# Odd mixer: stacked running sums for the decay rows, one exponential a head, sums of squares tile by tile

## The reference

```python
# Conformer: val * sigmoid(gate), causal conv of 31 taps, layer norm over 512 channels, silu
u = _causal_dwconv(val * jax.nn.sigmoid(gate), conv_w, conv_b)
return jax.nn.silu(_layer_norm(u, ln_g, ln_b))

# Mamba-2 SSD: 16 heads of 64 in 2 groups, chunks of 128 tokens
a_cum = jnp.cumsum(dt_c * a_head.reshape(G, HG), axis=2)
seg = a_cum[:, :, :, None] - a_cum[:, :, None, :]
decay_ls = jnp.exp(jnp.where(causal, seg, -jnp.inf))
cb = jnp.einsum('bclgn,bcsgn->bclsg', c_c, b_c)
y_diag = jnp.einsum('bclsgh,bcsghp->bclghp', cb[..., None] * decay_ls, xdt)
...
y_off = jnp.einsum('bclgn,bcghpn,bclgh->bclghp', c_c, prev, jnp.exp(a_cum))
y = (y_diag + y_off) + d_skip * xs
y = y * jax.nn.silu(z)
yg = yg * lax.rsqrt(jnp.mean(jnp.square(yg), axis=-1, keepdims=True) + LN_EPS)   # per group of 512
```

## Time and profile before

| | us |
|---|---|
| median of 3 runs | 1790.54 (1789.36 to 1792.71) |
| the profiled execution | 1790.46 |
| its span | 1788.4 |
| PE busy (matmul) | 1684.4, 94% |
| DVE, ACT, POOL busy | 1015.6, 739.4, 139.2 |
| mean granted TensorE clock | 0.968 of 2.4 GHz |

### The profile page before, as it was taken

The page is one execution under the profiler, slowest core; times in us unless marked ns, Lnnn a source line. Parts: engine busy times, 40 slices in busy tenths (PEclk is TensorE's granted clock), DMA queues, the critical chain, the costliest instruction groups (busy, mean ns, idle before and its releaser), DMA issues.

```text
span 1788.4 us, 26739 instructions
## 1 busy us (share of the span) xinstructions
PE 1684.4 (94%) x10986; PEld 1397.2 (78%) x10986; DVE 1015.6 (57%) x1276; ACT 739.4 (41%) x1019; POOL 139.2 (8%) x155
## 2 busy tenths in 40 slices
PE   7998998989899999999998989899998999999996
PEld 6777897778677888888776766688887788888885
DVE  4589564664666543434488864455636755434346
ACT  4544543363425232324267744523634441423231
POOL 5110110000000000000025620000000000000000
PEclk9998999999999999999999999799999999999998
DMA  5220002344022333233232220053530233333231
GB/s 193 71 83 25 4 4 97 130 131 129 25 94 87 103 94 100 91 105 118 83 130 79 86 71 12 1 189 94 156 104 22 96 96 105 95 95 104 88 127 59
DMA packets 41161, 159.73 MB, mean 89 GB/s; under 512 B 4560, under 2 KB 4688, under 8 KB 39632
## 3 DMA queue, kind: packets, MB, share of 16 engines
q1 hardware_dynamic: 41040, 158.03, 28.1%
HBM read 153.81 MB, written 4.19 MB: 88 GB/s over the span
## 4 chain that ended last, share of the span: by engine, by line
PE 80%; DVE 13%; ACT 4%; issue 2%; DMA 0%; POOL 0%; SPq 0%; DVEq 0%; ACTq 0%; POOLq 0%
PE bank L569 24%; PE bank L571 23%; PE bank L570 23%; DVE w_lo L1664 2%; DVE h L1680 1%; PE bank L731 1%; PE bank L1067 1%; DVE nbh L1725 1%; PE bank L941 1%; DVE act_lo L1677 1%; ACT w_hi L1194 1%; PE bank L750 1%; PE bank L744 1%; DVE sconv L1680 1%; DVE lnst L1993 1%
## 5 line engine op out<-in xcount | busy, mean ns | idle before, releaser
L1664 DVE TENSOR_TENSOR w_lo<-w_raw,w_hi 128x1024 fp32r<-128x1024 f32 x263 | 326.8, 1244 | 312.5 <-ACT w_hi L1194 309.8
L569 PE MATMUL bank<-act_lo,w_hi 128*128 128x512 f32 x1048 | 418.1, 399 | 31.8 <-DVE w_lo L1664 16.2
L1194 ACT ACTIVATE w_hi<-w_raw 128x1024 fp32r<-128x1024 f32 x263 | 278.9, 1061 | 361.5 <-PE bank L571 347.4
L570 PE MATMUL bank<-act_hi,w_lo 128*128 128x512 f32 x1048 | 413.0, 394 | 0.0
L571 PE MATMUL bank<-act_hi,w_hi 128*128 128x512 f32 x1048 | 412.7, 394 | 0.0
L569 PEld LDWEIGHTS bank<-act_lo,w_hi 128*128 128x128 f32 x1048 | 200.2, 191 | 80.6 <-issue 18.0
L570 PEld LDWEIGHTS bank<-act_hi,w_lo 128*128 128x128 f32 x1048 | 200.2, 191 | 42.3 <-issue 1.2
L571 PEld LDWEIGHTS bank<-act_hi,w_hi 128*128 128x128 f32 x1048 | 199.9, 191 | 42.5
L569 PE MATMUL bank<-w_lo,aux_hi 128*128 128x512 f32 x576 | 224.5, 390 | 5.3 <-DVE act_lo L1677 5.3
L570 PE MATMUL bank<-w_hi,aux_lo 128*128 128x512 f32 x576 | 224.2, 389 | 0.0
L571 PE MATMUL bank<-w_hi,aux_hi 128*128 128x512 f32 x576 | 224.1, 389 | 0.0
(11 more groups left out here) (355 smaller groups left out, 2087.5 us busy)
## 6 DMA issues: line engine op xcount, KB each, us to landing
w_raw<-weights SPq DMA_DIRECT2D x263, 512.0 KB, 3.6
gb<-ln_rows SPq DMA_DIRECT2D x6, 1024.0 KB, 5.8
stage<-x_feat SPq DMA_DIRECT2D x4, 512.0 KB, 6.0
h<-x_tok SPq DMA_DIRECT2D x1, 2048.0 KB, 8.7
stage<-mem_feat SPq DMA_DIRECT2D x2, 1024.0 KB, 5.7
spill<-h SPq DMA_DIRECT2D x1, 2048.0 KB, 7.2
h<-spill SPq DMA_DIRECT2D x1, 2048.0 KB, 7.9
out<-h SPq DMA_DIRECT2D x4, 512.0 KB, 2.6
```

What stands on the lines that cost most here:

```text
L569: pe.matmul(o, whi, xlo, start=first, stop=False)
L570: pe.matmul(o, wlo, xhi, start=False, stop=False)
L1194: act.activation(w_hi[:, s], w_raw[:, s], ACT.Copy).then_inc(S("w_hi_done"), 1)
L1664: dve.tensor_tensor(w_lo[:, s], w_raw[:, s], f(w_hi[:, s]), ALU.subtract).then_inc(S("w_split"), 1)
```

## The change

The decay rows: the mask aside, one product per chunk of 128 tokens makes `a_cum[l] - a_cum[s]` at once. `from_sums` and `to_sums` hold the sums' high and low parts and constants stacked on 112 partitions; `head_row` (ACT) picks one head by a 0/1 scale per partition (`heads16`) into `head_sums`. One exponential of 512 columns per head then does. Rows go two pairs ahead of the scores. The sums of squares come tile by tile: the conformer's inside chunk 28 (`inside`, after every second of its eight pieces), the SSD's one pair behind the scores. `crb` follows pair 0, `conf_norm` (DVE) follows pairs 1 and 2, `conf_gate` (ACT) pairs 5 to 7. The output projection takes its inputs in another order (`SLOT1`, with the weight chunks in `SOURCE` to match), the first SSD group before the conformer. In the input projection the scan, `dt_tokens`, the four-instruction exponential block and the channel mean change their turns.

```diff
...
+                    12: [("free cacc", 0)], 15: [("stok", 2)], 16: [("free cacc", 1)], 18: [("slast", 1)],
                     20: [("sxt", 2)], 21: [("free cacc", 2), ("sxt", 2)], 22: [("sxt", 2)], 23: [("sxt", 2)],
-                    24: [("sbt", 2), ("scb", 2)], 25: [("free cacc", 3), ("sst", 2), ("cmean", 1)],
-                    26: [("sst", 2), ("yoff", 2)], 27: [("sst", 2), ("csum", 1)], 28: [("yoff", 2), ("crb", 1), ("sbc0", 2)]}
+                    24: [("sbt", 2), ("scb", 2)], 25: [("sst", 2)], 26: [("free cacc", 3), ("sst", 2), ("cmean", 1), ("yoff", 2)],
+                    27: [("sst", 2)], 28: [("yoff", 2)]}
...
-        TILES += [("yoff", 2)]
...
-        TILES += [("out1", 4), ("rsum1", 1), ("rbc1", 1), ("out1", 4)]
+            TILES += [(f"sbc{_h + 2}", 2)] * (_h < 6) + [(f"sy{_h}", 1)]
+            TILES += [("crb", 1)] * (_h == 0) + [("rsum", 1)] * (_h in (1, 5)) + [("rbc0", 1)] * (_h == 6)
+            TILES += [("free rsum", 0)] * (_h == 6)
+        TILES += [("out1", 4), ("rbc1", 1), ("free rsum", 1), ("out1", 4)]
...
-        acum_hi = sb("acum_hi", [16, T], F32R, at=aux_at + 12288)
-        acum_lo = sb("acum_lo", [16, T], F32R, at=aux_at + 14336)
+        HK = 112
+        from_sums = sb("from_sums", [HK, T], F32R, at=aux_at + 12288)
+        to_sums = sb("to_sums", [HK, T], at=aux_at + 14336)
+        sums_hi = sb("sums_hi", [16, T], F32R, at=aux_at + 8 * PW * 4)
+        head_sums = [sb("head_sums01", [HK, 2, T], F32R, at=after_p1 + 4 * (CP + T) * 4 + 8192),
+                     sb("head_sums23", [HK, 2, T], F32R, at=lru_at)]
+        SLOT1 = [4, 5, 6, 7, 0, 1, 2, 3, 8, 9, 10, 11]
...
+                if j == 2:
+                    pool.wait_ge(S("cval_out"), 4)
+                    pool.memset(to_sums[:], -1.0).then_inc(S("masks"), 1)
+                    pool.tensor_copy(from_sums[:], ones[0:HK, 0:1].to_broadcast([HK, T])).then_inc(S("masks"), 1)
...
                     hd = 2 * hp + q
+                    pe.wait_ge(S("s_head"), hd + 1)
                     o = take(f"sbc{hp}", q)
-                    head = identr[0:16, hd:hd + 1].to_broadcast([16, P])
-                    pe.matmul(o[:], head, acum_hi[:], start=True, stop=False)
-                    pe.matmul(o[:], head, acum_lo[:], start=False, stop=False)
-                    pe.matmul(o[:], identr[:], causalr[:], start=False, stop=True).then_inc(S("mixer_mm"), 1)
-
-            def token_sums(name, tiles):
-
-                o = take(name, 0)
+                    to_head = head_sums[hp % 2]
+                    for c in range(NSC):
+                        cols = slice(c * SC, c * SC + SC)
+                        pe.matmul(o[:, cols], from_sums[:, cols], to_head[:, q, cols], start=(c == 0), stop=False,
+                                  skip_group_check=True)
+                    pe.matmul(o[:], identr[:], causalr[:], start=False, stop=True, skip_group_check=True)\
+                        .then_inc(S("mixer_mm"), 1)
+
...
                 for c in range(NSC):
-                    for j in range(4):
-                        last = pe.matmul(o[:, c:c + 1], tiles(j)[:, c * SC:c * SC + SC], ones[:, 0:1], start=(j == 0),
-                                         stop=(j == 3))
-                last.then_inc(S("mixer_mm"), 1)
+                    last = pe.matmul(o[:, c:c + 1], tile[:, c * SC:c * SC + SC], ones[:, 0:1],
+                                     start=(first and c == 0), stop=(j == 3), skip_group_check=True)
...
+            def square_sums(hp):
+
+                g, j = divmod(hp, 4)
+                if j == 0:
+                    take("rsum", g)
+                pe.wait_ge(S("s_ysq"), hp + 1)
+                last = token_sums(bank("rsum", g), p1[:, XS + hp, PAD:PW], j, j == 0)
+                if j == 3:
+                    last.then_inc(S("rsum_mm"), 1)
...
             def at_26():
                 chunk_states(1)
+                channel_mean()
                 from_states(1)
...
+            def variance(k):
+
+                if k % 2:
+                    if k == 1:
+                        take("csum", 0)
+                    pe.wait_ge(S("c_sq"), k // 2 + 1)
+                    last = token_sums(bank("csum", 0), csq[:, k // 2], k // 2, k == 1)
+                    if k == KD - 1:
+                        last.then_inc(S("mixer_mm"), 1)
...
+            def odd_mixer():
+
+                from_states(3)
                 pe.wait_ge(S("masks"), 2)
                 decay_rows(0)
-
-            def odd_mixer():
-
-                from_states(3)
+                decay_rows(1)
                 for hp in range(8):
-                    if hp < 7:
-                        decay_rows(hp + 1)
+                    if hp < 6:
+                        decay_rows(hp + 2)
...
-                    if hp == 4:
-                        square_sums(0)
+                    if hp == 0:
+                        pe.wait_ge(S("c_rstd"), 1)
+                        across_features("crb", CROOT)
+                    if hp:
+                        square_sums(hp - 1)
...
-                                  between={13: dt_tokens, 18: dt_last, 20: lambda: values_to_tokens(0),
...
-                                           23: lambda: values_to_tokens(3), 24: keys_to_tokens, 25: at_25, 26: at_26,
-                                           27: at_27, 28: at_28}, place=PLACE1)
+                                           23: lambda: values_to_tokens(3), 24: keys_to_tokens, 25: lambda: chunk_states(0),
+                                           26: at_26, 27: lambda: chunk_states(2), 28: lambda: from_states(2)},
+                                  inside={28: variance}, place=PLACE1)
...
-                            between={2: lambda: square_sums(1), 4: lambda: square_roots(1)} if l else {3: even_back},
-                            slot=range(12) if l else SLOT0)
+                            between={1: lambda: square_sums(7), 5: lambda: square_roots(1)} if l else {3: even_back},
+                            slot=SLOT1 if l else SLOT0)
...
+            def head_row(hp):
+
+                if hp >= 2:
+                    act.wait_ge(*made("sbc", 2 * hp - 2))
+                else:
+                    act.wait_ge(S("masks"), 2)
+                for q in range(2):
+                    hd = 2 * hp + q
+                    done(act.activation(head_sums[hp % 2][:, q], to_sums[:], ACT.Copy, scale=heads16[0:HK, hd:hd + 1]),
+                         "s_head")
+
...
+                if i == 22:
+                    act.wait_ge(S("s_alo"), 1)
+                    step(act.activation(to_sums[0:16], sums_hi[:].bitcast(F32), ACT.Copy))
+                    step(act.activation(from_sums[64:80], sums_hi[:].bitcast(F32), ACT.Copy))
+                    done(act.activation(from_sums[96:112], to_sums[32:48], ACT.Copy), "s_sums")
...
-                if i == 19:
...
+                if i == 22:
...
+                if i == 27:
+                    head_row(0)
+                    head_row(1)
...
-                    for c in range(NSC):
-                        cols = slice(c * SC, c * SC + SC)
-                        at = NEGATED + 16 * c + n
-                        ins = act.activation(mt(n)[:, cols], bank(f"sbc{hp}", n % 2)[:, cols], ACT.Exp,
-                                             bias=small[:, at:at + 1])
-                        if c == NSC - 1:
-                            done(ins, "sbc_out")
+                    done(act.activation(mt(n), bank(f"sbc{hp}", n % 2)[:], ACT.Exp), "sbc_out")
...
+            done(act.activation(small[:, CROOT:CROOT + 4], bank("csum", 0)[:, 0:4], ACT.Sqrt, bias=eps[:, 0:1],
+                                scale=1.0 / 512), "csum_out")
+            for hp in range(2):
+                decays(hp)
+                head_row(hp + 2)
...
+            def conf_gate(j):
...
             for hp in range(8):
                 if hp < 6:
                     decays(hp + 2)
+                if hp < 4:
+                    head_row(hp + 4)
                 act.wait_ge(S("s_y"), hp + 1)
                 done(act.activation(p1[:, XS + hp, PAD:PW], p1[:, ZS + hp, PAD:PW], ACT.Square), "s_ysq")
                 if hp == 5:
                     root(0)
+                if hp >= 5:
+                    conf_gate(hp - 5)
             mix_hi(4, 8)
             split(FIRST["out1"] + 1 + W_SLOTS)
             root(1)
+            conf_gate(3)
...
-                at = [0, 0, 0, 3, 8, 13, 18, 23, 28, 33]
-                return at[i] if i < 10 else min(33 + 2 * (i - 9) if i < 22 else 57 + 5 * (i - 21), 4 * DVE_TAPS)
+                at = [0, 0, 0, 3, 8, 13, 18, 23, 28, 31]
+                return at[i] if i < 10 else min(31 + 2 * (i - 9) if i < 22 else 55 + 4 * (i - 21), 4 * DVE_TAPS)
...
-                if i in (10, 14, 19, 23):
-                    conf_sum((10, 14, 19, 23).index(i))
-                if i == 10:
+                if i in (10, 14, 20, 24):
+                    conf_sum((10, 14, 20, 24).index(i))
```

(37 more changed lines are left out.)

84 lines of the change are left out of this document (34 added, 50 removed).

## The result

The changed kernel takes 1776.07 us (median, 1773.76 to 1777.01) against 1791.2 of the kernel before beside it: ratio 0.9913, interval 0.9901 to 0.9924, so it is 14 to 18 us faster. The forecast was 1772.1, the range 1762 to 1784. Its profiled execution took 1773.76, with a span of 1772.0 and a mean clock of 0.975.

A forecast was written before the change was run, and what follows sets the result against it. TensorE was 80% of the last-ending chain; late VectorE and ScalarE, one-column work and the slow clock cost time besides. Gains 5.0 (7.0 - 2.0) + 7.0 + 4.1 + 2.3 = 18.4 off 1790.5 give 1772.1 us, range 1762 to 1784.

The forecast's parts named there:

- the five waits that the forecast named: TensorE waits: chunk 21 (4 to 5 us), chunk 24 (2), `head_sums` (2.4), `crb` marker (3.9), output projection's start (4.8).
- last chunk ended near 1094: Sign that the forecast is right: the input projection's last chunk ends near 1094 us, for 1106.4 before.
- The output projection's start: Sign that the forecast is right: the output projection starts near 1150 us, for 1166.1 before.
- Chunks 13 to 20: Input projection: earlier ScalarE splits and the moved exponential block gain 7.0 us at the chunk-21 restart, bounds 4.3 and 8.
- Chunks 22 to 24: Input projection: ScalarE's and VectorE's fuller turns cause a new wait before chunk 24, cost 2.0 us.
- To the end of the projection: Chunk 24 to the input projection's end: `crb` and decay rows move behind, cheaper sums, no slow clock; 7.0 us less.
- The mixer: Input projection's end to output projection: cheaper decay rows, three idle times, slow clock; 55.7 us for 59.8, 4.1 less.
- Output projection: Fewer sums of squares and `rbc1` moved, against slow clock behind the idle time: 2.3 us less.
- A: Rival: the clock holds in the mixer, idle times cost no slow clock; 6.6 us more gained, 1765.5; chance 0.15.
- B: Rival: ScalarE and GpSimd pace chunks 13 to 20, chunk 24's wait eats the 5.0 gain; 1777.1 us; chance 0.14.
- C: Rival: the decay rows' 112-row stationaries cost a tile change, 6.4 us more, 1778.5; chance 0.12.
- D: Rival: TensorE stays at 1.2 GHz through the mixer to the output projection; slower, 1799.5 us; chance 0.10.

The follow-up runs named there:

- y_block19: The changed kernel with ScalarE's table load and three small exponentials back in turn 19, the copies staying in turn 22; 1773.52 us, ratio 0.9904.
- x_copies25: The changed kernel with ScalarE's three copies into the stacks in turn 25 rather than 22; 1770.49 us, ratio 0.9881.
- y_bunch28: The changed kernel with the conformer's 32 one-column steps in one go behind the first eighth of chunk 28; 1778.79 us, ratio 0.9927.
- x_crbnorm: The changed kernel with all four products of the conformer's norm behind pair 1, freeing the bank of `crb` one pair earlier; 1771.25 us, ratio 0.9886.

## Why the prediction was right, and where it was off

The mechanism came mostly as written: the five waits that the forecast named are all there, two of them shorter (before chunk 21, 3.50 for 4 to 5 and without its slow clock; on `head_sums`, 1.37 for 2.4). The sum was 4.8 too large (18.4 for 13.6 behind the origin). Part of the closeness of the total is luck, since the profiled execution was 2.8 us ahead before the change began. The sign "last chunk ended near 1094" came true (1094.43) only by that: from the origin the forecast was 196.3, and T is 199.1. The output projection's start (1151.50, near 1150) is the same case.

- **Chunks 13 to 20**, 7.0 forecast, 4.2 measured: the term that was mis-sized, and the largest miss. I let ScalarE's splits "come some 1.8 to 2.6 us earlier" because the scan and the small steps went elsewhere. They went to other turns of the same ring. The sign was a wait before chunk 21 that starts 5 us earlier; it starts 1.5 earlier from the origin (128.6 for 130.0). VectorE's splits of turns 13 and 19, before and then after, show it:

```profile
985.37 1.23 DVE L1664 TENSOR_TENSOR w_lo<-w_raw,w_hi 128x1024 fp32r<-128x1024 f32 x1 [0.34 <-ACT w_hi L1194]
...
1021.18 1.22 DVE L1664 TENSOR_TENSOR w_lo<-w_raw,w_hi 128x1024 fp32r<-128x1024 f32 x1 [0.50 <-ACT w_hi L1194]
```

```profile
983.78 1.23 DVE L1712 TENSOR_TENSOR w_lo<-w_raw,w_hi 128x1024 fp32r<-128x1024 f32 x1 [0.34 <-ACT w_hi L1223]
...
1018.51 1.23 DVE L1712 TENSOR_TENSOR w_lo<-w_raw,w_hi 128x1024 fp32r<-128x1024 f32 x1
```

  With origins 2.8 apart the first is 1.2 later after, and the second is level (123.1 and 123.2 from the origin), so all that was gained at chunk 21 came behind it, around the block: 2.0 by its move (y_block19), the rest by what fits the 1.85 us wait for `stm` and the fourth exponential. The lower bound of 4.3 was the right value. The new wait at chunk 12 belongs here as well: I had the old one of 3.8 go to a later chunk.
- **Chunks 22 to 24**, 2.0 lost as forecast in the wait (2.01), and the wait goes when either the copies (x_copies25) or the block (y_block19) leaves ScalarE's turn 22. Net 1.3 are lost from restart to the end of chunk 24, since no slow stretch followed the shorter restart wait, where before 6.8 us of it did.
- **To the end of the projection**, 7.0 forecast, 6.3 measured. Bursts take 0.79 each, 3.2 for 2.8. They held the clock, as said. The parts fit: 0.9 of `crb` and 2.2 of rows went behind T, and the bursts in place of one go are worth 3.4 (y_bunch28), 6.5 together.
- **The mixer**, 4.1 forecast, 2.6 measured. Waits 10.6 (1.37, 4.02, 0.26, 4.99) for 11.1. The slow clock, 6.6 forecast (2.4 behind the first wait, 4.2 behind the second), cost 3.5 (against y_block19) and 3.0 (x_crbnorm): the sum came right, the shares did not, and the first share is one that y_block19 doesn't pay at all. What was too small is plain work, 40.0 for 38.0: a head's row is 0.68 for 0.65, and a whole pair of rows, scores, carry and sum of squares 4.63 at the full clock for 4.4 (from 1129.47 to 1134.10 of the changed kernel). The working also took the 27 us at 0.50 of before as three spells of 9 us; they are 13.6, 10.1 and 3.4 (mean clocks of 0.66 over 1120 to 1140, 0.72 over 1140 to 1158, 0.86 over 1158 to 1170).
- **Output projection**, 2.3 forecast, 1.8 measured.

Of the rivals, A is out: two slow stretches stayed (mixer). B is partly true: the ring paces chunks 13 to 20, and the wait at chunk 24 ate what the block's move had gained there, but 2.9 of the 5.0 forecast are left at the end of chunk 24. C is out: 112 rows cost no tile change, 0.10 a step. D is out: the clock came back after 6.8 us each time.

By the rule of the Trainium skill's page "TensorE: Matmul & The Clock Gate" (Part 3, The mechanism) each of the 64 steps would have taken 0.05 us more than the 0.10 forecast, an estimate of the prediction. The trace has 0.10 and does not agree with the rule.

## What to carry to other kernels

Where two engines pass work to each other in a ring, moving a step to another turn of it gained nothing here (the scan) or nearly nothing (the block); moving one to a turn that had room for it did gain (the copies, 2.1 us). And the work of the engine that looks busiest may lie in a shadow, as the taps did. Read which bank a product will take before handing it out: a norm that ended one pair late made TensorE wait 4 us for a bank and run at 1.2 GHz for 7 more. Short one-column steps did best between dense products in small bursts. And compare two profiles from a place ahead of the change, since 2.8 us of difference here were there before it.

## What the runs showed that was not expected

Small steps of VectorE got longer where they were moved next to GpSimd's sums. Before, `stm` (128x64) took 0.23 us with GpSimd idle; after, in turn 18, it stands inside a run of GpSimd's adds (VectorE, then GpSimd, of the changed kernel):

```profile
1017.67 0.81 DVE L1725 TENSOR_TENSOR stm<-stm 128x64 f32<-128x64 f32 x1
```

```profile
1014.35 4.05 POOL L562 TENSOR_TENSOR cacc<-cacc,cprod 128x512 f32<-128x512 f32 x3 [3.05 <-ACT cprod L1525]
```

It ended with that add (1018.4), 0.58 later than alone. Ahead of the scan two small steps took 1.17 and 1.40 us in turn 9, beside adds from 958.84 to 963.2, against 0.68 and 0.48 before, with GpSimd idle; the scan itself took 1.21 both times. The Trainium skill's page "SBUF — State Buffer" (SBUF: two separate sides) calls the port pair of the two engines an exclusive lock, held for a whole instruction, on which the other blocks; these rows agree, at 0.5 to 0.9 us for a step of 0.2 to 0.7. Not every step is blocked: three convolution steps that read a bank took 2.30 us from 966.80, beside adds that ran from 963.61 to 969.38, and 2.31 elsewhere. So a cheap step has no fixed price in such a ring.

The other is that the same wait of 1.37 us was followed by 7 or 3.4 us at 1.2 GHz in kernels that are equal up to there, and by none in y_block19, which differs only in turn 19 of the input projection, some 75 us earlier. A single profiled execution can't put a price under about 4 us on such a wait.
